# Mixer decay matrices from one spread matrix product and a ScalarE relu, causal mask moved into the scores, and the first norm's sums inside the first dense tile

## The chip, the cores and the metric

The kernel runs on one core of a Trainium2 chip. The core has TensorE (matrix products, in the profile PE, with its weight loads as PEld), VectorE (DVE), ScalarE (ACT) and GpSimd (POOL); each runs its own instruction list and waits for the others by semaphores. SyncE (SP) issues most DMAs. The metric is device time of one launch in microseconds (us), lower is better.

## The reference

One layer of a hybrid decoder: an RMSNorm, one wide input projection that feeds three branches, a gated merge, and a convolutional feed-forward. There are 512 prompt tokens and 8 x 8 sample tokens, so 576 columns in all. The change touches the first norm, the step sizes `dt` and the state-space mixer (branch a), which works in chunks of 128 tokens (the 64 sample tokens are a fifth, narrower chunk) for 32 heads in 8 groups of 4:

```python
def _rmsnorm(x, w):
    y = xf * lax.rsqrt(jnp.mean(xf * xf, axis=-1, keepdims=True) + RMS_EPS)
    return (y * w.astype(jnp.float32)).astype(x.dtype)

dt = jax.nn.softplus(dt_raw.astype(jnp.float32) + lw["dt_bias"].astype(jnp.float32))
a = -jnp.exp(lw["a_log"].astype(jnp.float32))
cs = jnp.cumsum((dt * a).reshape(b, c, chunk, h), axis=2)
seg = cs[:, :, :, None, :] - cs[:, :, None, :, :]
lmat = jnp.exp(jnp.where(causal[None, None, :, :, None], seg, -jnp.inf)).reshape(b, c, chunk, chunk, g, r)
cb = jnp.einsum("bcign,bcjgn->bcijg", cc, bc)
y_diag = jnp.einsum("bcijgr,bcjgrp->bcigrp", cb[..., None] * lmat, xdt)
```

Here i is the receiving token and j the source token. Because `dt * a` is negative, `cs` falls along a chunk, so `cs_i - cs_j` is at most 0 wherever j is at or before i.

## The kernel before

Features lie on the 128 partitions and tokens on the columns. Every projection is cut into dense tiles: 128 output features, 1024 inputs in 8 pieces of 128, 576 tokens in two halves of 288. Each fp32 operand is split in a high and a low part, so a tile is 48 matmuls of 288 columns (`pe_dense`; L208 and L213 where all pieces stand ready, L228 where it goes piece by piece). GpSimd splits the streamed weights (L2627, L2631), paced by the end of earlier tiles.

The order of work on each engine is written out by hand; there is no scheduler. TensorE's list is: the sums of the first norm, the step-size stage `pe_dt`, then the mixer.

**First norm and first tile.** ScalarE and GpSimd square the eight pieces of x. With `alone=5`, TensorE sums five squared pieces one by one and then the sum `acc` of the other three, which VectorE adds up (L385, L389): 30 products with one moving column (L287). The mean and its root follow on VectorE and ScalarE. The first dense tile (the step sizes) works on unnormed rows `y_hi`, `y_lo` and is scaled afterwards by the spread root (`pe_spread`, L310); `act_copied` (L375) and `dve_scaled` (L370) wait for the tile's end, and VectorE makes the normed rows only after that (L412, L365).

**Step-size stage.** VectorE computes `dt` and `dt * a`, lays the latter out for the cumulative sums (five copies, L1155), then runs the first convolutions (L920). TensorE makes the cumulative sums (L1073); ScalarE copies them into `cs_row` and `cs_lhs` (L1098, L1099), and VectorE subtracts to get their low parts (L1168, L1169). Then convolutions and SiLUs go on; the last SiLU (L936) frees the first chunk on TensorE (L551).

**Mixer.** For each of 8 groups G there are six slots. Slot k on TensorE is: a dense tile for the next group, from k = 2 on a state product (`pe_round`, L624), the products of chunk k (`pe_chunk_out`, L574 to L599), then the preparation of chunk k+1 (`pe_chunk`). The chunks of a group are `STEPS = (0, CH, 1, 2, 3)`, where CH is the narrow sample chunk. The preparation makes the scores and transposes in psA (L551 to L554), and, in two PSUM banks psL and psE of the tile psLE:

```python
            if c > 0:
                if s == 2:
                    pe.wait_ge(ysb_ready, G + 1)
                pe.matmul(per_head(psE[:, 0:GH * m]), ones_top[:], cs_rhs[:, :, 0:m], start=True, stop=True)
            late = late_p if c < CH else late_s
            pe.matmul(per_head(psL[0:m, 0:GH * m]), cs_lhs[:, at], cs_rhs[:, :, 0:m], start=True, stop=False)
            pe.matmul(per_head(psL[0:m, 0:GH * m]), eye_r[0:m, 0:m], over_heads(late[0:m, 0:m], m, m),
                      start=False, stop=True).then_inc(le_full, 1)
```

psE is cs_i spread over the partitions (L562), psL is cs_i - cs_j (L564) plus a large negative number where j is later than i (L565). On ScalarE a slot is: a copy (L714), the Exp of psL (L716) and of psE (L718), `act_rhs` for the next chunk (four copies with a per-partition scale, L706), the copies and first tap of a convolution (L751 to L756, L763), its tanh (L771). On VectorE: the chunk's outputs (L893 to L905), the scaled inputs (L871, L872), Exp times scores (L876), Exp times C (L880), the decay of sample states (L987), the convolution (L920), the state addition `dve_round` (L993), a SiLU (L935, L936). The banks psL and psE also take the state product L624, so `pe_chunk` waits for `n_free`, which L993 raises, ahead of the first matmul into them.

## Time and profile before

| | us |
|---|---|
| median of 3 runs | 1792.97 (1792.79 to 1794.67) |
| the profiled execution, its own time | 1796.09 |
| its span, first to last instruction | 1794.0 |
| TensorE busy | 1733.1 (97%) |
| VectorE busy | 939.3 (52%) |
| ScalarE busy | 621.0 (35%) |
| GpSimd busy | 977.2 (54%) |

The span is what the trace covers; 2.1 us of the execution's own time lie around it. Busy time is that of instructions, and a matmul's end is modelled, so neighbouring matmuls overlap in the rows: what one costs is the distance from its start to the next start. The mean granted TensorE clock was 0.986 of full speed. In a timeline row, "x4" merges four instructions in a row, and the bracket is the idle time ahead of it with what ended it.

### The profile page before, as it was taken

Reading aid. Unit: us, or ns where it says so; the run is one execution under the profiler, and the core shown is the slowest. Engines: PE = TensorE matmul, PEld = TensorE weight load, DVE = VectorE, ACT = ScalarE, POOL = GpSimd, SP = SyncE. Lnnn points to the kernel's source line nnn. Section 1 sums busy time; section 2 is a strip of 40 time slices with the busy share of each in tenths; the row PEclk is TensorE's granted clock in tenths of the full one; section 3 lists DMA queues with packets and bytes.
Section 4 is the critical chain, followed back from the end, with each engine's and each line's share of the span. In section 5 each row is a group of like instructions: output and inputs, shape, how many; then the busy total and the mean of one; then the engine's idle time right before and its main releaser. Section 6 shows DMA issues by size and latency. Waiting matters only on the chain.

```text
span 1794.0 us, 35603 instructions
## 1 busy us (share of the span) xinstructions
PE 1733.1 (97%) x13875; PEld 1603.1 (89%) x13875; DVE 939.3 (52%) x1584; ACT 621.0 (35%) x1660; POOL 977.2 (54%) x1088
## 2 busy tenths in 40 slices
PE   7899999999999999998998999999999999999997
PEld 7798898999898999786777998879998999999997
DVE  6766677631775424766664732222246651662454
ACT  3455555523554201555442112320124430331231
POOL 5535454555445466221553544236676876886775
PEclk9899999999999999999999999999999999999998
DMA  4212322313133223113895265532221222223223
GB/s 142 92 48 98 109 77 81 109 60 121 60 103 104 90 88 117 48 48 107 298 303 213 75 237 206 189 123 83 83 83 61 82 90 79 81 82 91 74 83 109
DMA packets 53605, 198.48 MB, mean 111 GB/s; under 512 B 6353, under 2 KB 7378, under 8 KB 49874
## 3 DMA queue, kind: packets, MB, share of 16 engines
q1 hardware_dynamic: 41762, 134.32, 22.9%
q10 hardware_dynamic: 7056, 46.85, 7.1%
q0 software_dynamic: 4640, 15.21, 2.6%
q8 instruction: 110, 1.80, 0.4%
q14 instruction: 37, 0.30, 0.1%
HBM read 180.43 MB, written 15.92 MB: 109 GB/s over the span
## 4 chain that ended last, share of the span: by engine, by line
PE 87%; DVE 6%; DMA 2%; ACT 2%; issue 1%; POOL 0%; SPq 0%; DVEq 0%; POOLq 0%; ACTq 0%
PE dps L208 36%; PE dps L213 18%; PE dps L228 14%; DMA pages<-kv_pages_dram 2%; PE psY L574 1%; PE psLE L1688 1%; PE psLE L624 1%; PE psY L591 1%; PE psY L287 1%; PE psLE L2135 1%; PE psY L1412 1%; PE psLE L2097 1%; DVE cout L920 1%; PE psY L1711 1%; PE psA L1402 1%
## 5 line engine op out<-in xcount | busy, mean ns | idle before, releaser
L2631 POOL TENSOR_TENSOR w_lo<-w_raw,w_hi 128x256 fp32r<-128x256 f32 x800 | 699.3, 905 | 16.7
L2627 POOL TENSOR_SCALAR w_hi<-w_raw 128x1024 fp32r<-128x1024 f32 x200 | 218.9, 1094 | 651.3 <-PE dps L213 385.2
L208 PE MATMUL dps<-xn_hi,w_hi 128*128 128x288 f32 x1504 | 323.3, 297 | 3.0 <-ACT cbuf L756 1.9
L208 PE MATMUL dps<-xn_lo,w_hi 128*128 128x288 f32 x1504 | 325.0, 298 | 0.0
L208 PEld LDWEIGHTS dps<-xn_hi,w_hi 128*128 128x128 f32 x1504 | 247.0, 190 | 6.0 <-POOL w_hi L2627 2.1
L208 PEld LDWEIGHTS dps<-xn_lo,w_hi 128*128 128x128 f32 x1504 | 241.5, 189 | 0.0
L213 PE MATMUL dps<-xn_hi,w_lo 128*128 128x288 f32 x1504 | 215.7, 296 | 0.0
L213 PEld LDWEIGHTS dps<-xn_hi,w_lo 128*128 128x128 f32 x1504 | 205.7, 189 | 0.0
L208 PE MATMUL dps<-y_lo,w_hi 128*128 128x288 f32 x824 | 177.9, 298 | 0.0
L208 PE MATMUL dps<-y_hi,w_hi 128*128 128x288 f32 x824 | 177.1, 297 | 0.5 <-POOL w_hi L2627 0.5
L228 PE MATMUL dps<-xn_hi,w_hi 128*128 128x288 f32 x624 | 144.5, 313 | 5.3 <-DVE xn_lo L365 4.5
L208 PEld LDWEIGHTS dps<-y_hi,w_hi 128*128 128x128 f32 x824 | 134.5, 190 | 0.9 <-POOL w_hi L2627 0.8
L228 PE MATMUL dps<-xn_hi,w_lo 128*128 128x288 f32 x624 | 134.8, 298 | 0.0
L228 PE MATMUL dps<-xn_lo,w_hi 128*128 128x288 f32 x624 | 134.3, 297 | 0.0
L208 PEld LDWEIGHTS dps<-y_lo,w_hi 128*128 128x128 f32 x824 | 132.9, 189 | 0.0
L228 PEld LDWEIGHTS dps<-xn_hi,w_hi 128*128 128x128 f32 x624 | 100.0, 191 | 30.2 <-issue 20.9
L213 PE MATMUL dps<-y_hi,w_lo 128*128 128x288 f32 x824 | 118.5, 296 | 0.0
L213 PEld LDWEIGHTS dps<-y_hi,w_lo 128*128 128x128 f32 x824 | 112.7, 189 | 0.2 <-POOL w_lo L2631 0.2
L920 DVE SCALAR_TENSOR_TENSOR cout<-cbuf,fea,cout 128x600 f32<-128x600 f32 x96 | 84.3, 879 | 42.1 <-ACT cout L763 39.6
L228 PEld LDWEIGHTS dps<-xn_lo,w_hi 128*128 128x128 f32 x624 | 101.6, 191 | 0.0
L228 PEld LDWEIGHTS dps<-xn_hi,w_lo 128*128 128x128 f32 x624 | 101.3, 190 | 0.0
L2514 DVE SCALAR_TENSOR_TENSOR fout<-fin,fea,fout 128x592 f32<-128x592 f32 x44 | 48.4, 1100 | 91.4 <-ACT fout L2500 91.4
(417 smaller groups left out, 2816.7 us busy)
## 6 DMA issues: line engine op xcount, KB each, us to landing
w_raw<-wstream_dram SPq DMA_DIRECT2D x209, 512.0 KB, 3.5
pages<-kv_pages_dram SPq DMA_DIRECT2D x70, 256.0 KB, 3.9
pages<-kv_pages_dram POOLq DMA_DIRECT2D x58, 256.0 KB, 4.1
st_in<-state_t_dram ACTq DMA_DIRECT2D x8, 1024.0 KB, 5.0
ssm_s_dram<-st_in ACTq DMA_DIRECT2D x8, 1024.0 KB, 4.3
kc<-mem_kt_dram ACTq DMA_DIRECT2D x4, 2048.0 KB, 7.9
vc<-mem_v_dram ACTq DMA_DIRECT2D x3, 2048.0 KB, 7.8
w_more<-wstream_dram SPq DMA_DIRECT2D x8, 512.0 KB, 3.8
```

Source lines behind the costliest of these rows:

```text
L208: pe.matmul(dps[:, par, b, 0:cw], w_hi[:, par, k * P:(k + 1) * P], a[:, k, c0:c0 + cw], start=(k == 0 and j == 0), stop=False)
L213: mm = pe.matmul(dps[:, par, b, 0:cw], w_lo[:, par, k * P:(k + 1) * P], hi[:, k, c0:c0 + cw], start=False, stop=(k == nk - 1))
L228: mm = pe.matmul(dps[:, par, b, 0:cw], w, a[:, k, c0:c0 + cw], start=(k == 0 and j == 0), stop=(k == nk - 1 and j == 2))
L287: mm = pe.matmul(psY[:, c * kinds + kind:c * kinds + kind + 1], squares[:, r], ones[:, 0:1], start=True, stop=True)
L574: pe.matmul(o, xdt[0:m, h * 64:h * 64 + 64], lv[:, h, :], start=True, stop=not carried)
L591: pe.matmul(psY[:, 256:512], btok[:], xdtd[:], start=True, stop=True).then_inc(y_full, 1)
L624: mm = pe.matmul(psLE[:, half, 0:256], bm[rows, half * 4 + r, :], xds[rows, :], start=True, stop=True)
L920: ins = dve.scalar_tensor_tensor(co, cb[:, j:j + CW - PAD], w(j), co, ALU.mult, ALU.add)
L1402: mm = pe.transpose(turn_bank(n)[:, k * P:(k + 1) * P], probs(i)[:, hh, kt * P:(kt + 1) * P], ident)
L2514: link(dve.scalar_tensor_tensor(fo, fb[:, 1:1 + FO], tap_of("fconvw", p, u, 1, FCONV), fo, ALU.mult, ALU.add))
L2627: pool.tensor_scalar(w_hi[:, par, :], w_raw[:, par, :], 1.0, 1.0, ALU.mult, ALU.mult).then_inc(w_hi_done, 1)
L2631: ins = pool.tensor_tensor(w_lo[:, par, at], w_raw[:, par, at], w_hi[:, par, at].bitcast(F32), ALU.subtract)
```

## The change

It does three things.

In the mixer, `cs_lhs`, the matrix `late` and its identity `eye_r` go away. Only psE is made, for every chunk. ScalarE forms `relu(cs_j - cs_i)` for each of the four heads, with psE as input, scale -1 and the source token's sum `cs_tok` as per-partition bias, waits for itself (`act_step`), and takes Exp with scale -1 in place. Tokens j later than i come out as some number up to 1, and the causal mask is multiplied into the scores on VectorE (`scores`), which the product with the four heads then reads instead of psA. The rows 64 to 127 of `cs_rhs` are set once to zero instead of once a group.

In the step-size stage, the layout copy becomes one copy of half the columns, the copies and subtractions for `cs_lhs` go away, and TensorE and ScalarE make `cs_tok`, two products and two copies.

In the first norm, `alone` is 2 instead of 5: VectorE adds up six squared pieces, the first two additions ahead of its first rows, and TensorE's sum over `acc` stands inside the first dense tile after its second piece; the spread stands after the sixth piece instead of the fifth. VectorE's constants, of which five go away, are made after the rows instead of first.

```diff
@@ norm_stage: pe_sums, dve_f
                 for k in range(alone):
-                    if k in POOL_SQUARED:
-                        pe.wait_ge(norm_lo_pool, k - POOL_SQUARED[0] + 1)
-                    else:
-                        pe.wait_ge(sq_ready, at["sq_ready"] + k + 1)
+                    pe.wait_ge(sq_ready, at["sq_ready"] + k + 1)
                     sums_of(pe, sq[:, k, :], k)
+                if not rows:
+                    pe_sum_last(pe)
+
+            def pe_sum_last(pe):
                 pe.wait_ge(sq_used, at["sq_used"] + adds)
                 sums_of(pe, acc, alone).then_inc(sum_full, 1)
...
                 if rows:
+                    dve.wait_ge(sq_ready, alone + 1)
+                    add(3)
+                    add(4)
                     dve_row_low(dve, 0)
                     dve_row_low(dve, 1)
                     dve_first_low(dve)
...
+                    for k in range(X_FIRST, KT):
+                        add(k)
+                    for k in range(2, 5):
+                        dve_row_low(dve, k)
...
@@ pe_chunk
-            if c > 0:
-                if s == 2:
-                    pe.wait_ge(ysb_ready, G + 1)
-                pe.matmul(per_head(psE[:, 0:GH * m]), ones_top[:], cs_rhs[:, :, 0:m], start=True, stop=True)
-            late = late_p if c < CH else late_s
-            pe.matmul(per_head(psL[0:m, 0:GH * m]), cs_lhs[:, at], cs_rhs[:, :, 0:m], start=True, stop=False)
-            pe.matmul(per_head(psL[0:m, 0:GH * m]), eye_r[0:m, 0:m], over_heads(late[0:m, 0:m], m, m),
-                      start=False, stop=True).then_inc(le_full, 1)
+            if s == 2:
+                pe.wait_ge(ysb_ready, G + 1)
+            pe.matmul(per_head(psE[:, 0:GH * m]), ones_top[:], cs_rhs[:, :, 0:m], start=True, stop=True).then_inc(le_full, 1)
@@ act_rhs, act_chunk
-            if s == 0:
-                act.activation(cs_rhs[64:P, :, :], spread(sel[64:P, group_heads(G)], 64, P), ACT.Copy)
+            if n == 0:
+                act.activation(cs_rhs[64:P, :, :], over_heads(ones[64:P, :], 64, P), ACT.Copy, scale=0.0)
...
-            ins = act.activation(l_exp[0:m, 0:GH * m], psL[0:m, 0:GH * m], ACT.Exp)
+            for h in range(GH):
+                at_h = slice(h * m, h * m + m)
+                ins = act.activation(l_exp[0:m, at_h], psE[0:m, at_h], ACT.Relu, bias=cs_tok[0:m, c, G * GH + h:G * GH + h + 1], scale=-1.0)
+            chains["act"](ins)
+            ins = act.activation(l_exp[0:m, 0:GH * m], l_exp[0:m, 0:GH * m], ACT.Exp, scale=-1.0)
@@ dve_chunk
+            causal = c_("upto_p") if c < CH else c_("upto_s", TS)
+            link(dve.tensor_tensor(scores[0:m, 0:m], psA[0:m, 384:384 + m], causal, ALU.mult))
             dve.wait_ge(exp_ready, n + 1)
             lv = per_head(l_exp[0:m, 0:GH * m])
-            ins = dve.tensor_tensor(lv, lv, over_heads(psA[0:m, 384:384 + m], m, m), ALU.mult)
+            ins = dve.tensor_tensor(lv, lv, over_heads(scores[0:m, 0:m], m, m), ALU.mult)
@@ pe_dt
-            pe_dense(pe, first, y_hi, y_lo, ready=rows_ready, part=(0, 5))
+            pe_dense(pe, first, y_hi, y_lo, ready=rows_ready, part=(0, 2))
+            norm1.pe_sum_last(pe)
+            pe_dense(pe, first, y_hi, y_lo, ready=rows_ready, part=(2, 6))
             norm1.pe_spread(pe)
-            pe_dense(pe, first, y_hi, y_lo, ready=rows_ready, part=(5, KT))
+            pe_dense(pe, first, y_hi, y_lo, ready=rows_ready, part=(6, KT))
...
+            pe.matmul(psL[:, 256:384], c_("upto_p"), da, start=True, stop=True)
+            pe.matmul(psL[0:TS, 384:416], c_("upto_s", TS), dt_tok[0:TS, 1, CH, :], start=True, stop=True)
@@ act_dt
-            for dst, r0 in ((cs_row[:], 0), (cs_lhs[64:P, :], 64)):
-                act.activation(dst[:, 0:SEQ], psY[r0:r0 + 64, :], ACT.Copy)
-                act.activation(dst[:, SEQ:T], psA[r0:r0 + 64, cs_tail], ACT.Copy).then_inc(cs_hi, 1)
+            act.activation(cs_row[:, 0:SEQ], psY[0:64, :], ACT.Copy)
+            act.activation(cs_row[:, SEQ:T], psA[0:64, cs_tail], ACT.Copy).then_inc(cs_hi, 1)
+            act.activation(cs_tok[:, 0:CH, :].rearrange("p c h -> p (c h)"), psL[:, 256:384], ACT.Copy)
+            chains["act"](act.activation(cs_tok[0:TS, CH, :], psL[0:TS, 384:416], ACT.Copy))
@@ dve_dt
-            for c in range(CH + 1):
-                p = P if c < CH else TS
-                four = dt_tok[0:p, 1, c, :].rearrange("p (o h) -> p o h", o=1).to_broadcast([p, 4, HEADS])
-                dve.tensor_copy(da_rows[0:p, c * P:(c + 1) * P].rearrange("p (o h) -> p o h", o=4), four)
+            dve.tensor_copy(da_rows.rearrange("p (c o h) -> p c o h", c=CH + 1, o=2),
+                            dt_tok[:, 1, :, :].rearrange("p c (o h) -> p c o h", o=1).to_broadcast([P, CH + 1, 2, HEADS]))
...
-            dve.wait_ge(cs_hi, 2)
-            for low, r0 in ((cs_row, 32), (cs_lhs, 96)):
-                part = low[r0:r0 + 32, :]
-                dve.tensor_tensor(part[:, 0:SEQ], psY[r0:r0 + 32, :], part[:, 0:SEQ].bitcast(F32), ALU.subtract)
-                ins = dve.tensor_tensor(part[:, SEQ:T], psA[r0:r0 + 32, cs_tail], part[:, SEQ:T].bitcast(F32), ALU.subtract)
-            ins.then_inc(cs_done, 1)
+            dve.wait_ge(cs_hi, 1)
+            low = cs_row[32:64, :]
+            dve.tensor_tensor(low[:, 0:SEQ], psY[32:64, :], low[:, 0:SEQ].bitcast(F32), ALU.subtract)
+            dve.tensor_tensor(low[:, SEQ:T], psA[32:64, cs_tail], low[:, SEQ:T].bitcast(F32), ALU.subtract).then_inc(cs_done, 1)
```

The diff moves instructions at three places. First, on TensorE from its first matmul: L287 is a sum over one squared piece or over `acc`, L228 the first dense tile. Before:

```order
L287 MATMUL psY<-cst,norm_sq 128x1 x25
L287 MATMUL psY<-cst,norm_acc 128x1 x5
L228 MATMUL dps<-y_hi,w_hi 128x288 x2
L228 MATMUL dps<-y_lo,w_hi 128x288 x2
L228 MATMUL dps<-y_hi,w_lo 128x288 x2
L228 MATMUL dps<-y_hi,w_hi 128x288 x2
L228 MATMUL dps<-y_lo,w_hi 128x288 x2
L228 MATMUL dps<-y_hi,w_lo 128x288 x2
```

After the change:

```order
L287 MATMUL psY<-cst,norm_sq 128x1 x10
L228 MATMUL dps<-y_hi,w_hi 128x288 x2
L228 MATMUL dps<-y_lo,w_hi 128x288 x2
L228 MATMUL dps<-y_hi,w_lo 128x288 x2
L228 MATMUL dps<-y_hi,w_hi 128x288 x2
L228 MATMUL dps<-y_lo,w_hi 128x288 x2
L228 MATMUL dps<-y_hi,w_lo 128x288 x2
L287 MATMUL psY<-cst,norm_acc 128x1 x5
L228 MATMUL dps<-y_hi,w_hi 128x288 x2
```

Fifteen of the thirty one-column sums are gone, and the five over `acc` stand behind the tile's first two pieces.

Second, on TensorE and ScalarE in the mixer, at the third chunk of a group. L551 to L554 (then L560 to L563) fill psA, L562 (then L570) is psE. TensorE before:

```order
L551 MATMUL psA<-feat 128x128
L553 MATMUL psA<-cst,feat 128x128 x2
L554 MATMUL psA<-cst,feat 128x128
L562 MATMUL psLE<-cs_rhs,ones_top 128x512
L564 MATMUL psLE<-cs_rhs,cs_lhs 128x512
L565 MATMUL psLE<-late_p,eye_r 128x512
L208 MATMUL dps<-xn_hi,w_hi 128x288 x2
```

TensorE after the change:

```order
L560 MATMUL psA<-feat 128x128
L562 MATMUL psA<-cst,feat 128x128 x2
L563 MATMUL psA<-cst,feat 128x128
L570 MATMUL psLE<-cs_rhs,ones_top 128x512
L208 MATMUL dps<-xn_hi,w_hi 128x288 x2
L208 MATMUL dps<-xn_lo,w_hi 128x288 x2
```

The two products into psL are gone and the next dense tile follows psE. ScalarE at the same chunk, before:

```order
L714 ACTIVATE btok<-psA 128x128
L716 ACTIVATE l_exp<-psLE 128x512
L718 ACTIVATE e_exp<-psLE 128x512
L706 ACTIVATE cs_rhs<-cs_row,sel 64x128 x4
L751 ACTIVATE cbuf<-dps 128x288
```

ScalarE after the change:

```order
L718 ACTIVATE btok<-psA 128x128
L722 ACTIVATE l_exp<-psLE,cs_tok 128x128 x4
L724 ACTIVATE l_exp<-l_exp 128x512
L726 ACTIVATE e_exp<-psLE 128x512
L710 ACTIVATE cs_rhs<-cs_row,sel 64x128 x4
L759 ACTIVATE cbuf<-dps 128x288
```

One Exp has become four relus and an Exp, all ahead of the Exp of psE and of the copies for the next chunk.

Third, on VectorE in the step-size stage, from `dt * a` (into `dt_tok`) to the first SiLU. Before:

```order
L1127 TENSOR_TENSOR dt_tok<-dt_tok,feat 128x160
L1155 COPY yg<-dt_tok 128x128 x4
L1155 COPY yg<-dt_tok 64x128
L1156 TENSOR_TENSOR ysb<-dt_tok,cst 64x256
L920 SCALAR_TENSOR_TENSOR cout<-cbuf,fea,cout 128x600 x6
L935 SCALAR_TENSOR_TENSOR feat<-cth,cout 128x512
```

After the change:

```order
L1136 TENSOR_TENSOR dt_tok<-dt_tok,feat 128x160
L1161 COPY yg<-dt_tok 128x320
L1163 TENSOR_TENSOR ysb<-dt_tok,cst 64x256
L930 SCALAR_TENSOR_TENSOR cout<-cbuf,fea,cout 128x600 x6
L945 SCALAR_TENSOR_TENSOR feat<-cth,cout 128x512
L946 SCALAR_TENSOR_TENSOR feat<-cth,cout 128x64
```

Five copies have become one of 320 columns, ahead of the six convolution steps.

## Rows read from the trace of the kernel before

**Rows 1.** The page: busy time by engine; the chain that ended last.

```profile
PE 1733.1 (97%) x13875; PEld 1603.1 (89%) x13875; DVE 939.3 (52%) x1584; ACT 621.0 (35%) x1660; POOL 977.2 (54%) x1088
...
PE 87%; DVE 6%; DMA 2%; ACT 2%; issue 1%; POOL 0%; SPq 0%; DVEq 0%; POOLq 0%; ACTq 0%
```

**Rows 2.** Timeline of TensorE around one chunk: start, length (us), instruction.

```profile
166.22 0.48 PE L562 MATMUL psLE<-cs_rhs,ones_top 128*128 128x512 f32 x1
...
176.19 0.48 PE L562 MATMUL psLE<-cs_rhs,ones_top 128*128 128x512 f32 x1
176.50 0.40 PE L564 MATMUL psLE<-cs_rhs,cs_lhs 128*128 128x512 f32 x1
176.74 0.39 PE L565 MATMUL psLE<-late_p,eye_r 128*128 128x512 f32 x1
176.97 0.42 PE L208 MATMUL dps<-xn_hi,w_hi 128*128 128x288 f32 x2
```

**Rows 3.** Waits of TensorE, whole span: us in total, times, longest.

```profile
PE psA L551 <- DVE feat L936: 6.1, 1, 6.1
...
PE dps L208 <- ACT cbuf L756: 1.9, 1, 1.9
```

**Rows 4.** Timeline of ScalarE, same step, part.

```profile
166.50 0.28 ACT L714 ACTIVATE btok<-psA 128x128 f32<-128x128 f32 x1 [3.31 <-PE psA L554]
167.20 0.60 ACT L716 ACTIVATE l_exp<-psLE 128x512 f32<-128x512 f32 x1 [0.42 <-PE psLE L565]
...
168.17 1.28 ACT L706 ACTIVATE cs_rhs<-cs_row,sel 64x128 fp32r<-64x128 f32 x4
...
170.37 0.89 ACT L763 ACTIVATE cout<-cbuf,fea 128x600 f32<-128x600 f32 x1
```

**Rows 5.** Timeline of VectorE, same step, part.

```profile
171.37 2.60 DVE L920 SCALAR_TENSOR_TENSOR cout<-cbuf,fea,cout 128x600 f32<-128x600 f32 x3 [0.98 <-ACT cout L763]
174.23 0.69 DVE L993 TENSOR_TENSOR st_in<-st_in,psLE 128x512 f32<-128x512 f32 x1 [0.26 <-PE psLE L624]
```

**Rows 6.** Timeline of TensorE from its first work to the second dense tile, part.

```profile
9.02 10.80 PE L287 MATMUL psY<-cst,norm_sq 128*128 128x1 f32 x50 [9.02 <-ACT norm_sq L325]
...
21.81 0.83 PE L228 MATMUL dps<-y_hi,w_hi 128*128 128x288 f32 x2
...
23.39 0.68 PE L228 MATMUL dps<-y_hi,w_hi 128*128 128x288 f32 x2
23.87 0.68 PE L228 MATMUL dps<-y_lo,w_hi 128*128 128x288 f32 x2
...
27.34 1.45 PE L310 MATMUL psLE<-cst,norm_rs 128*128 128x128 f32 x12
...
31.06 0.43 PE L208 MATMUL dps<-y_hi,w_hi 128*128 128x288 f32 x2
```

**Rows 7.** Timeline of VectorE in the same stretch, part.

```profile
13.83 1.97 DVE L1111 TENSOR_TENSOR w_lo<-w_raw,w_hi 128x1024 fp32r<-128x1024 f32 x1 [1.02 <-POOL w_hi L2685]
15.72 1.27 DVE L385 TENSOR_TENSOR norm_acc<-norm_sq 128x576 f32<-128x576 f32 x1
```

**Rows 8.** Timeline of VectorE in the step-size stage, part.

```profile
56.38 3.17 DVE L1155 COPY yg<-dt_tok 128x128 f32<-128x128 f32 x5
...
71.85 0.68 DVE L1168 TENSOR_TENSOR cs_row<-psY,cs_row 32x512 fp32r<-32x512 f32 x1 [0.86 <-ACT cs_lhs L1099]
...
72.68 0.70 DVE L1168 TENSOR_TENSOR cs_lhs<-psY,cs_lhs 32x512 fp32r<-32x512 f32 x1
...
73.55 3.45 DVE L920 SCALAR_TENSOR_TENSOR cout<-cbuf,fea,cout 128x600 f32<-128x600 f32 x3
```

**Rows 9.** Timeline of ScalarE in the step-size stage, part.

```profile
71.11 0.59 ACT L1098 ACTIVATE cs_lhs<-psY 64x512 fp32r<-64x512 f32 x1
```

**Rows 10.** Two stretches: length, busy time by engine, granted clock (PEclk), DMA share, GB/s.

```profile
73.70:80.40 6.70, 6.62 (x48) 6.41 (x48) 5.49 (x7) 2.00 (x3) 3.90 (x4) 1.00 0.22 66
86.40:89.75 3.35, 3.29 (x12) 3.09 (x13) 2.60 (x6) 1.24 (x4) 0.00 (x0) 0.50 0.49 157
```

59 lines of the change are left out of this document (26 added, 33 removed).

## Prediction

> **What bounds the kernel now.** I read the page first. TensorE is busy for 97% of the span, and 87% of the chain that ended last is TensorE's [rows 1]. So an instruction taken out of its list is worth its spacing, as long as nothing else becomes the last to be ready. The timeline of TensorE around one chunk shows the price: the two products into psL start at 176.50 and 176.74 and the next dense tile at 176.97, with no idle time noted, so 0.47 us for both. The same chunk step one slot earlier started at 166.22, this one at 176.19: a slot lasts 9.97 us [rows 2].
>
> The list of TensorE's waits has two long ones before the mixer's steady part: 6.1 us for VectorE's last SiLU (L936) and 1.9 us for a ScalarE copy (L756) [rows 3]. There VectorE and ScalarE set the time, not TensorE, and what counts is what leaves their lists. In the mixer I then read ScalarE and VectorE over the same slot, for the room that they have behind TensorE [rows 4, 5], and the start of all engines [rows 6, 7].
>
> **Mixer, TensorE.** Wide chunks 1 to 3 lose both products into psL: 24 times 0.47 = 11.3 us. Chunk 0 loses two and gains psE, so one: 8 times 0.23 = 1.8 us. The narrow chunk loses two of 256 columns; I have no row for these here, so the bounds are 0 and the 0.47 of the wide ones, and I take 0.40, near the wide ones, since a weight load stands with each: 8 times 0.40 = 3.2 us (0 to 3.8). Sum: 16.3 us.
>
> **Mixer, ScalarE.** The price is four relus with a per-partition bias and a wait, ahead of Exp. No relu is in the trace. The nearest row is L706, four 128-column activations with a per-partition scale: 1.28 us from the first start to the last end [rows 4]. A relu reads PSUM, L706 reads SBUF; L714, 128 columns out of PSUM without a per-partition operand, took 0.28 us, so PSUM is not dear. As bounds I take 0.28 us for the four together, as if they overlapped into one, and 0.60 us for each, the price of L716 at four times the width. I take 1.28 us, since L706 shares width and kind of operand.
>
> Let T be the start of psE (166.22 in the slot shown). L714 ends at T+0.56, the relus at T+1.84, the in-place Exp starts at T+1.87. The two Exps took 0.97 us together (167.20 to 168.17), so L706 starts at T+2.84, where before it started at T+1.95: ScalarE is 0.9 us later against psE. Behind it, L763 ended at T+5.04 (170.37+0.89) and now ends at T+5.93; the convolution L920 waits for it and started 0.1 us later; its three steps of 2.60 us end at T+8.63, and L993 (0.69 us), which stands behind it on VectorE, ends at T+9.33. The next psE waits for L993. Before, L993 ended at 174.92 and psE came at 176.19: 1.27 us of room [rows 2, 5]. After, psE would come at T+9.97-0.47 = T+9.50: 0.2 us of room, 0.1 with the way of a semaphore. This holds in slots 2 and 3 of the seven groups that have convolutions, so 14 times. The removed work thus fits, but only just: I put 1.0 us of loss in the sum, and the bounds are 0 (room kept) and, at 0.60 us a relu, 2.40-1.28-0.1 = 1.0 us, 14 times, 14 us.
>
> The masked scores on VectorE are one 128x128 product. They stand ahead of VectorE's wait for Exp, which now comes 0.9 us later, so they cost nothing; if ScalarE were early, they would cost at most as much as the state addition on 512 columns, 0.69 us, in 40 chunks, on an engine with time to spare at most of them. The product of scores and Exp stays as wide as it was. The zero rows of `cs_rhs` made once instead of eight times and the five constants off VectorE's list lie beside other work; I give them nothing. SP's and GpSimd's queues keep their order, and no DMA moves.
>
> **Step-size stage.** Five copies of 128 columns took 3.17 us [rows 8], 0.63 each. One of 320 columns, half as many elements, costs 1.6 us at the same rate; it costs no less than one of the five, 0.63 us. GpSimd works beside it as before, so part of the price is per instruction: I take 1.0 us, a gain of 2.2 us (1.6 to 2.5). ScalarE's copy for `cs_lhs` at 71.11 stood ahead of VectorE's subtraction at 71.85, which waited 0.86 us for it [rows 8, 9]: 0.74 us goes. The second pair of subtractions, 72.68 to the convolution at 73.55, goes: 0.87 us. The new copies of `cs_tok` stand behind the signal `cs_hi`, and the tanh behind them is not awaited for several us. Sum: 3.8 us (3.2 to 4.1). All of it reaches TensorE, since it waits 1.9+6.1 = 8.0 us there and its two added products, four instructions at the 1.45 us of the twelve of the spread [rows 6], take 0.5 us of that.
>
> The Trainium skill (VectorE: DVE Perf Modes, "Side-by-side: where the cycles go") counts a single-source copy in SBUF at two elements a cycle plus about 158 cycles at 0.96 GHz. By it the five copies would be an estimated 5 times 0.23 = 1.2 us and the new one 0.33 us, a gain of 0.8 us and a sum lower by 1.4 us. The trace has 3.17 us for the five, so I go by the row.
>
> **First norm.** The first dense tile now waits for w_lo (L1111, ends at 15.80 [rows 7]) instead of the thirty sums, so it starts at 15.8 instead of 21.81 [rows 6]. Two pieces, 12 matmuls, at the spacing of the first rows (0.48 us a pair, 0.24 each) end at 18.7. VectorE adds three pieces from 15.8 at 1.2 us each (L385 took 1.27), so `acc` is there at 19.5. Five sums are ten instructions at 10.80/50 = 0.216 us: until 21.7. So the sum, and the mean, come as late as before; what is gained is the two pieces already done and the spread at a better place.
>
> Then 36 matmuls and the spread remain. Before, 48 and a spread of about 1.4 us took 9.25 us (21.81 to 31.06). A matmul of the tile costs 0.24 us at the slow spacing and 0.138 at the fast one (6.62 us for 48 [rows 10]; a pair lasts 0.68 us at 23.39 and 0.43 at 31.06 [rows 6]), so about 12 of the 48 were slow, although TensorE had been busy with one-column sums since 9.02. I take it that 12 are slow again after the sums: 2.9+24 times 0.138+1.4 = 7.6 us, so the tile ends at 29.3 and with a short wait for rows at 29.5, a gain of 1.5 us. Bounds: all 36 fast, 6.4 us, gains 2.9; all slow with the spread doubled, 11.4 us, loses 2.0. The tile's end carries on undiminished, because `act_copied` and `dve_scaled` wait for it and VectorE's normed rows stand behind.
>
> **Sum.** 1.5+3.8+16.3-1.0 = 20.6 us. Against the profiled execution's 1796.09 that is 1775.5; its time was 3.1 us above the median of the runs, so for a median I forecast 1772.4, say 1772.
>
> **Rivals.** A change within 0.2% (3.6 us) is about what a measurement of this kernel cannot tell from none.
>
> *A. ScalarE's loop binds.* If a relu takes 0.42 us, four take 1.68 instead of 1.28, and the loop is 0.3 us over TensorE's slot. If slot 1, where eight masked copies and the copy of psE to `ysb` stand behind the relus, is as tight, that is 21 places and 6.3 us, 5.3 more than in the sum: 1778. For it: the room is 0.1 us, a small difference of many rows. Against it: L706. Chance 0.22.
>
> *B. The clock.* After the 6.1 us wait, 86.40 to 89.75 ran at a granted clock of 0.50, the lower of its two levels (1.2 GHz); after the 1.9 us wait, 73.70 to 80.40 had 1.00 [rows 10]. The new wait ahead of the first chunk is 8.0-3.8-0.5 = 3.7 us, between them. If the clock stays up, 3.35/2 = 1.7 us more are gained, and if the first tile's 36 matmuls are fast too, 1.4 more: 1769. Against it: the first tile began slow behind 12 us of sums. Chance 0.15. The Trainium skill (TensorE: Matmul & The Clock Gate, "HAM oscillation") says that idle gaps between groups of matmuls bring the clock back to half; the two rows agree, and do not say where a gap of 3.7 us falls.
>
> *C. Slower.* The same loop, with dearer relus. To lose 20.6+1.0+3.6 = 25 us in 14 slots, each must be 1.8 us over, the four relus 3.2 us, 0.8 us each: 1797 or more. That is above the 0.60 us of an activation four times as wide. It takes a stall in PSUM that no row shows. Chance 0.03.
>
> *D. No change.* The removed products would have to be covered by other work. Only a loop 1.5 us over TensorE's slot gives that, 0.73 us a relu: 1793. Chance 0.03.
>
> **How the numbers follow.** The forecast itself has 0.55 (1769 to 1775), A 0.22, B 0.15, C and D 0.03 each, and 0.02 is left for a first tile that loses its 2.0 us. The range 1767.5 to 1780 takes in A and B with their bounds and leaves out C and D. Faster by over 0.2%: 0.94; within: 0.03; slower: 0.03.
>
> **What would show it.** Right: in the profile after, dense matmuls start within 0.3 us of psE's start, slots 2 and 3 of a group are about 9.5 us apart, no wait of TensorE for L993's successor sums to more than 2 us, and the wait for the last SiLU is 3 to 4.5 us. Wrong: TensorE waiting for the state addition or for `ysb` by tenths in every slot (A), relus above 0.4 us apart, or the second dense tile starting later than 31.06.

## The result and the profile after

The changed kernel took 1782.11 us (median of 15 runs, 1766.16 to 1787.84), the kernel before 1793.22 in the same session; the ratio is 0.9927, 95% interval 0.991 to 0.9945. So it is faster, by 10 to 16 us as the interval has it, and not by the 20.6 of the forecast: 1782 lies above the range of 1767.5 to 1780.

The profiled execution took 1780.18 us, its span is 1778.5. Its page, lines on busy time and on the chain, as [rows 1]:

```profile
PE 1712.6 (96%) x13777; PEld 1584.4 (89%) x13777; DVE 963.1 (54%) x1616; ACT 655.9 (37%) x1813; POOL 979.7 (55%) x1088
...
PE 78%; DVE 8%; ACT 7%; DMA 3%; issue 3%; POOL 0%; ACTq 0%; DVEq 0%; POOLq 0%; SPq 0%
```

TensorE's busy time fell by 20.5 us. That this is close to the forecast's 20.6 means nothing, since part of the latter are waits. TensorE's share of the chain that ended last fell from 87% to 78%, and ScalarE's rose from 2 to 7: part of the work taken away turned into waiting. TensorE's waits in the mixer (total, times, longest), to be held against [rows 3]:

```profile
PE psA L560 <- DVE feat L946: 4.4, 1, 4.4
PE psY L660 <- DVE l_exp L886: 2.4, 6, 0.4
PE psLE L570 <- DVE st_in L1003: 1.7, 9, 0.2
```

The 6.1 us wait is 4.4, the 1.9 us wait for `cbuf` is gone, and L660 is new: it is the row that TensorE spreads between two groups (`pe_grow`). Where the difference between the two profiles arises can be read from the first product of each of the 40 chunks. Chunk (0, 0) starts at 83.10 instead of 86.46, 3.4 us earlier; the last chunk at 582.11 instead of 591.58, 9.5 earlier, so the mixer gave 6.1 of the 15.3 forecast (the second profiles of the two kernels give 2.7 to 6.8 for it). The other 6.0 us of the two spans' difference arise behind the mixer, where nothing was changed: from the last chunk to the end it is 1202.4 us before and 1196.4 after. Over all profiles of this study with the whole work in them that stretch lies between 1189.9 and 1204.6 us, and the three with the mixer of before (1198 to 1203) lie inside the range of the others, so these 6.0 us cannot be put down to the change. A spread of 15 us there is wide enough for most of the 14 to 22 us over which the runs of one kernel lie, though only one run in each set was traced. Effects of 1 to 4 us are therefore read below from places in the traces and not from medians alone.

Distance from each chunk's first product to the next one's, in us, median over the groups, from the timelines (0-1 is chunk 0 to chunk 1, 4-0 is chunk 4 to the next group's chunk 0; chunks are numbered in the order of `STEPS`, so chunk 1 is the narrow one). The forecast is before less its own terms, 0.23, 0.40 for the narrow chunk and 0.47 three times, without the loss of 1.0 us in all:

```
                                        0-1    1-2    2-3    3-4    4-0
before                                11.16  10.30  10.03   9.98  17.06
forecast                              10.93   9.90   9.56   9.51  16.59
after                                 11.77   9.85   9.56   9.88  16.99
after, second profile                 11.79   9.72   9.56   9.87  16.99
one relu for four heads               12.68   9.71   9.57   9.50  16.70
GpSimd's split cut                    11.78   9.71   9.57   9.51  16.60
three edits of order                  11.16   9.71   9.57   9.50  16.69
those, and products of constants      12.67   9.71   9.57   9.50  16.69
those, and chunk 0's product twice    11.16   9.71   9.57   9.50  16.70
```

Chunk 2 to 3 came out to the hundredth and 1 to 2 within 0.1. The loss is in 0-1 (0.84 us a group against the forecast), 3-4 (0.37) and 4-0 (0.40). The theory with which the experiments began: 0-1 waits for ScalarE's longer chain at the group boundary, 3-4 and 4-0 for VectorE's taps (the three convolution steps of a slot), which now meet GpSimd. The rivals: ScalarE's relus alone hold all of them (the prediction's A), or it is chance of one execution.

### The profile page after: what moved, and what is told of

The parts are those of the page before. It is cut to its first block, busy times and chain, and to the rows that moved or that the text cites. A ratio compares the mean times of both kernels' runs of the same rounds, so it can differ in the third digit from the quotient of the medians.

```text
span 1778.5 us, 35636 instructions
## 1 busy us (share of the span) xinstructions
PE 1712.6 (96%) x13777; PEld 1584.4 (89%) x13777; DVE 963.1 (54%) x1616; ACT 655.9 (37%) x1813; POOL 979.7 (55%) x1088
## 4 chain that ended last, share of the span: by engine, by line
PE 78%; DVE 8%; ACT 7%; DMA 3%; issue 3%; POOL 0%; ACTq 0%; DVEq 0%; POOLq 0%; SPq 0%
PE dps L208 34%; PE dps L213 17%; PE dps L228 12%; DVE cout L930 2%; DMA ssm_p_dram<-state 1%; PE psLE L1693 1%; DMA pages<-kv_pages_dram 1%; ACT l_exp L722 1%; ACT cs_rhs L710 1%; PE psY L1417 1%; ACT cout L771 1%; PE psY L1716 1%; PE psLE L2140 1%; PE psA L1407 1%; PE psLE L2102 1%
## 5 line engine op out<-in xcount | busy, mean ns | idle before, releaser
L2636 POOL TENSOR_TENSOR w_lo<-w_raw,w_hi 128x256 fp32r<-128x256 f32 x800 | 697.4, 903 | 16.7
L2632 POOL TENSOR_SCALAR w_hi<-w_raw 128x1024 fp32r<-128x1024 f32 x200 | 223.5, 1117 | 634.8 <-PE dps L213 363.5
L228 PE MATMUL dps<-xn_hi,w_hi 128*128 128x288 f32 x624 | 143.5, 312 | 4.3 <-DVE xn_lo L363 3.9
L228 PE MATMUL dps<-xn_hi,w_lo 128*128 128x288 f32 x624 | 134.9, 298 | 0.0
L228 PE MATMUL dps<-xn_lo,w_hi 128*128 128x288 f32 x624 | 134.4, 297 | 0.0
L228 PEld LDWEIGHTS dps<-xn_hi,w_hi 128*128 128x128 f32 x624 | 100.3, 192 | 27.8 <-issue 20.9
L930 DVE SCALAR_TENSOR_TENSOR cout<-cbuf,fea,cout 128x600 f32<-128x600 f32 x96 | 104.6, 1090 | 31.4 <-ACT cout L771 28.9
L228 PEld LDWEIGHTS dps<-xn_hi,w_lo 128*128 128x128 f32 x624 | 101.5, 191 | 0.0
L228 PEld LDWEIGHTS dps<-xn_lo,w_hi 128*128 128x128 f32 x624 | 101.5, 191 | 0.0
```

The source lines that it names most:

```text
L228: mm = pe.matmul(dps[:, par, b, 0:cw], w, a[:, k, c0:c0 + cw], start=(k == 0 and j == 0), stop=(k == nk - 1 and j == 2))
L930: ins = dve.scalar_tensor_tensor(co, cb[:, j:j + CW - PAD], w(j), co, ALU.mult, ALU.add)
L2632: pool.tensor_scalar(w_hi[:, par, :], w_raw[:, par, :], 1.0, 1.0, ALU.mult, ALU.mult).then_inc(w_hi_done, 1)
L2636: ins = pool.tensor_tensor(w_lo[:, par, at], w_raw[:, par, at], w_hi[:, par, at].bitcast(F32), ALU.subtract)
```

## The experiments

Times are medians against the kernel before on the same chip; a ratio has its 95% interval. The runs lie on four chips, so medians are set against each other below only where they come from one.

| kernel | us | ratio to before |
|---|---|---|
| changed kernel again | 1783.93 | 0.9951 (0.9934 to 0.9969) |
| kernel before again (one run) | 1792.2 | |
| mixer part only | 1784.39 | 0.9971 (0.9947 to 0.9996) |
| first norm only | 1790.59 | 0.9995 (0.9973 to 1.0016) |
| products ahead of the first tile | 1779.76 | 0.9937 (0.9916 to 0.9959) |
| spread row waits for scores | 1785.76 | 0.9969 (0.9948 to 0.999) |
| copied rows late | 1779.13 | 0.9927 (0.9897 to 0.9957) |
| GpSimd's split cut (work left out) | 1763.14 | 0.9831 (0.9809 to 0.9853) |
| one relu (biases left out) | 1779.02 | 0.9912 (0.9883 to 0.9941) |
| three edits of order | 1777.06 | 0.9918 (0.9905 to 0.993) |
| those, and products of constants | 1775.43 | 0.9913 (0.9882 to 0.9944) |
| those, and chunk 0's product twice | 1774.53 | 0.9896 (0.9878 to 0.9914) |
| changed kernel, chunk 0's product twice | 1782.76 | 0.9943 (0.9924 to 0.9962) |

**The taps.** VectorE, GpSimd and TensorE of the changed kernel in slot 2 of group 2, timeline (start, length, instruction). VectorE:

```profile
227.38 3.26 DVE L930 SCALAR_TENSOR_TENSOR cout<-cbuf,fea,cout 128x600 f32<-128x600 f32 x3 [0.26 <-ACT cout L771]
230.56 0.67 DVE L1003 TENSOR_TENSOR st_in<-st_in,psLE 128x512 f32<-128x512 f32 x1
```

And GpSimd at the same time:

```profile
228.59 1.42 POOL L2632 TENSOR_SCALAR w_hi<-w_raw 128x1024 fp32r<-128x1024 f32 x1 [3.45 <-PE dps L213]
230.09 4.00 POOL L2636 TENSOR_TENSOR w_lo<-w_raw,w_hi 128x256 fp32r<-128x256 f32 x4
```

TensorE, with the psE of the slot before as its first line:

```profile
221.49 0.47 PE L570 MATMUL psLE<-cs_rhs,ones_top 128*128 128x512 f32 x1
...
230.97 0.27 PE L563 MATMUL psA<-cst,feat 128*128 128x128 f32 x1
231.38 0.47 PE L570 MATMUL psLE<-cs_rhs,ones_top 128*128 128x512 f32 x1
231.69 0.42 PE L208 MATMUL dps<-xn_hi,w_hi 128*128 128x288 f32 x2
```

The kernel before, GpSimd in the slot of [rows 5]:

```profile
173.78 1.10 POOL L2627 TENSOR_SCALAR w_hi<-w_raw 128x1024 fp32r<-128x1024 f32 x1 [4.61 <-PE dps L213]
```

The three taps take 3.26 us instead of the 2.60 of [rows 5]. In the kernel before they ended at 173.97, and GpSimd began its split at 173.78, when the third was under way; now they start later in the slot and the split, which follows the dense tile, starts earlier. The third tap, begun at 229.1, takes 1.50 us; the two ahead of it 0.84. What counts is which begins first: in the changed kernel's mixer all 28 taps that begin during a conversion `w_hi` take 1.50 to 1.58 us, and the 28 that are under way when one begins keep their 0.84. The addition L1003 then ends at 231.2, and psE, which waits for it, comes at 231.38, 0.41 us behind the transpose before it; in the kernel before the distance is 0.03. It is 0.40 to 0.43 in both slots 2 and 3 of all seven groups with convolutions, 14 places. The list of waits shows little of this, because it counts a wait from the modelled end of the matmul ahead; 1.2 of its 1.7 us for L570 are a wait of 0.2 us at six group boundaries, and the kernel before has these too.

Edit 1, ScalarE's copy of the next chunk's rows (L710, 1.2 us) behind the first tap in slots 2 and 3:

```diff
-            if k < 4:
+            if k < 4 and k not in (2, 3):
                 act_rhs(act, G, k + 1)
...
                     act_conv(act, N, k - 1)
+                if k in (2, 3):
+                    act_rhs(act, G, k + 1)
```

> The changed kernel, but in slots 2 and 3 of a group ScalarE copies the next chunk's rows (cs_rhs) behind the first tap of the convolution instead of ahead of it, so that VectorE's other three taps can start about 1.1 us earlier. Theory (the taps now start so late that they run beside GpSimd's split of the next weights, which stretches them from 2.60 to 3.26 us, and the addition behind them holds up TensorE's spread product): the taps take 2.6 us again, TensorE's wait of 0.37 us for the addition goes in slots 2 and 3, the distances of chunks 2 to 3 and 3 to 4 fall to about 9.2 and 9.5 us; some 5 us over the mixer, about 1777 us. Rival (GpSimd has no part in it, the taps are slower beside ScalarE's relus or by their own operands): the taps still take about 3.26 us wherever they start; the wait goes all the same since they start earlier. Second rival (the copied rows are now late instead): TensorE waits for cs_rhs, and the distances stay at 9.56 and 9.88.

Half of it came. 3-4 fell to 9.51 and 4-0 to 16.7, and the mixer shortened by 3.7 us (495.32 instead of 499.01 from the first chunk to the last). But the taps stayed long (3.3 us): against the chunk's start they begin only 0.4 us earlier (5.98 us behind it instead of 6.41), because VectorE itself is busy until then, and the third one still met the split. 2-3 had nothing to give, it stood at the forecast already. So the taps were moved enough to clear TensorE's wait, not enough to clear GpSimd, and this run alone does not tell the theory from the first rival.

Edit 2, the split itself:

```diff
+            full = D if first else 64
-            pool.tensor_scalar(w_hi[:, par, :], w_raw[:, par, :], 1.0, 1.0, ALU.mult, ALU.mult).then_inc(w_hi_done, 1)
+            pool.tensor_scalar(w_hi[:, par, 0:full], w_raw[:, par, 0:full], 1.0, 1.0, ALU.mult, ALU.mult).then_inc(w_hi_done, 1)
...
-                at = slice(piece * D // 4, (piece + 1) * D // 4)
+                at = slice(piece * full // 4, (piece + 1) * full // 4)
```

> The changed kernel with GpSimd's split of the streamed weights cut to 64 of 1024 columns behind the first two tiles: the high and low parts of the other columns stay those of an earlier tile, so most of that work is left out; every other instruction stays. Theory (the taps are stretched only where they meet GpSimd: 1.5 us beside the high part, 1.2 beside the low parts, 0.84 alone): all taps take 0.84 us, three of them 2.6, TensorE's wait for the addition behind them goes, chunk 3 to 4 falls from 9.88 to about 9.5 us and chunk 4 to the next chunk 0 from 16.99 to about 16.7; chunk 0 to 1 stays at 11.77 (that wait is ScalarE's). Rival (ScalarE's longer chain alone sets these slots, GpSimd has no part): the taps take 0.84 us but the distances stay at 9.88 and 16.99. Second rival (the taps are slow by themselves): they still take 1.5 us.

The taps from 83 to 600 us, all instructions of the line (minimum, median and maximum in ns, first and last start). The changed kernel:

```profile
L930 DVE SCALAR_TENSOR_TENSOR cout<-cbuf,fea,cout x84: 842/844/1580, 102.3 to 532.6; 128x600 f32<-128x600 f32 x84
```

With the split cut:

```profile
L930 DVE SCALAR_TENSOR_TENSOR cout<-cbuf,fea,cout x84: 842/844/860, 94.6 to 522.5; 128x600 f32<-128x600 f32 x84
```

Without GpSimd no tap is longer than 0.86 us, 3-4 is 9.51, 4-0 is 16.60, and 0-1 stays at 11.78. That is the theory in every row: the stretch is GpSimd's, and the boundary is not. (Its time, 1763, is that of a kernel with much of GpSimd's work gone and is no goal; chunk (0, 0) also came 5 us earlier, since VectorE's step-size stage meets the split too: its first six taps take 5.14 us without it, 7.31 with it.) The Trainium skill has the rule that the prediction should have weighed (GPSIMD Engine Reference, "1. Specifications"): GpSimd shares its way into SBUF with VectorE, and contends with instructions of VectorE with two inputs in SBUF. A tap has two, and the trace agrees with 0.84 us alone and 1.5 beside `w_hi`.

Edit 3, the other engine of the same loop, one relu of 512 columns for four:

```diff
-            for h in range(GH):
-                at_h = slice(h * m, h * m + m)
-                ins = act.activation(l_exp[0:m, at_h], psE[0:m, at_h], ACT.Relu, bias=cs_tok[0:m, c, G * GH + h:G * GH + h + 1], scale=-1.0)
-            chains["act"](ins)
+            chains["act"](act.activation(l_exp[0:m, 0:GH * m], psE[0:m, 0:GH * m], ACT.Relu, bias=cs_tok[0:m, c, G * GH:G * GH + 1], scale=-1.0))
```

> The changed kernel with one relu of 512 columns in place of four of 128, all with the first head's source sum as bias: the other three heads' biases are left out. Theory (ScalarE's longer chain is what holds the row between two groups, and it is only one of the two things that cost the later chunks): with some 0.5 us less of it, chunk 0 to 1 falls from 11.77 to about 11.3 us, chunk 3 to 4 stays at 9.8 or above since the taps still meet GpSimd's split, 4 us less at most and about 1780 us. Rival (the relus alone held the later chunks, GpSimd's part follows from them): chunk 3 to 4 falls to 9.5 and chunk 4 to the next 0 to 16.7 as well, about 1776 us.

Here the rival is borne out on the later chunks: 3-4 is 9.50 and 4-0 is 16.70 although taps still reach 1.57 us. So either half is enough: the loop is 0.4 us too long, GpSimd put 0.66 us into it and the relus 0.9, and whoever takes 0.4 out of it clears the wait. The wait at L660 went too (0.2 us in all). But 0-1 did not fall: it is 12.68 to 12.71 in all of groups 1 to 4, 6 and 7. Neither case expected that; it is taken up below.

**The group boundary.** The changed kernel between groups 1 and 2, timelines. ScalarE:

```profile
202.73 1.14 ACT L722 ACTIVATE l_exp<-psLE,cs_tok 128x128 f32<-128x128 f32 x4
203.88 1.28 ACT L724 ACT_TABLE_LOAD   x1
...
205.18 0.63 ACT L724 ACTIVATE l_exp<-l_exp 128x512 f32<-128x512 f32 x1
```

VectorE:

```profile
203.86 0.28 DVE L883 TENSOR_TENSOR scores<-psA,cst 128x128 f32<-128x128 f32 x1
205.91 0.69 DVE L886 TENSOR_TENSOR l_exp<-l_exp,scores 128x512 f32<-128x512 f32 x1 [1.77 <-ACT l_exp L724]
```

TensorE's first instruction of `pe_grow`:

```profile
206.75 0.62 PE L660 MATMUL psY<-cst,grs 128*128 128x128 f32 x4 [0.44 <-DVE l_exp L886]
```

The kernel before, ScalarE at such a boundary:

```profile
147.45 0.26 ACT L714 ACTIVATE btok<-psA 128x128 f32<-128x128 f32 x1
147.73 1.28 ACT L716 ACT_TABLE_LOAD   x1
...
149.03 0.60 ACT L716 ACTIVATE l_exp<-psLE 128x512 f32<-128x512 f32 x1
```

The square root of the group ahead makes ScalarE load the table of the exponential anew, before the change too. Now the four relus stand ahead of that load, so load and exponential come 1.1 us later, and L886 behind them signals `m_ready`, on which `pe_grow` waits. It waits only because psA, which it writes, was read last by that product; since the change the last reader is L883, done 2.4 us earlier.

```diff
-            link(dve.tensor_tensor(scores[0:m, 0:m], psA[0:m, 384:384 + m], causal, ALU.mult))
+            dve.tensor_tensor(scores[0:m, 0:m], psA[0:m, 384:384 + m], causal, ALU.mult).then_inc(a_neg, 1)
+            dve.wait_ge(a_neg, n + 2)
...
-                pe.wait_ge(m_ready, G * 5 + 6)
+                pe.wait_ge(a_neg, G * 5 + 7)
```

> The changed kernel, but the row that TensorE spreads between two groups (pe_grow) waits for the masked scores of the next chunk, the last reader of the psA bank, instead of for the finished products of that chunk (m_ready). Theory (the group boundary now waits for the longer ScalarE chain of relus, table load and exponential): TensorE's 0.6 us in front of that row goes in seven of eight groups, and the distance from chunk 0 to chunk 1 falls from 11.77 us to about 11.2; some 4 us over the mixer, so about 1778 us median against 1782 of the changed kernel. Rival (slot 0 is held by something behind that row too, the state's start or the normalised feature, which is equally late): the wait moves to the next instruction, the distance stays within 0.2 us of 11.77 and the time stays 1782.

0-1 fell to 11.17, as the theory has it, but 1-2 rose to 10.46, and the time did not fall. The two longest of TensorE's waits in its mixer:

```profile
PE psA L560 <- DVE feat L947: 4.4, 1, 4.4
PE psLE L614 <- DMA st_in<-state_t_dram: 4.4, 5, 1.8
```

The gain went one slot on: the states of the next group are loaded by a DMA that waits for the store of the old ones, and ScalarE issues that store behind chunk 0's relus, at 261.04 in this profile for the boundary whose chunk 0 began at 256.43 (in the kernel before at 147.40, where it began at 144.23). The third edit issues it ahead of the square root. The diff of that edit, run with the two others:

```diff
                 if G:
+                    act_state_out(act, G - 1)
                     act_root(act, G - 1)
...
-            if k == 0 and G:
-                act_state_out(act, G - 1)
```

> The changed kernel with three edits of order: the copied rows behind the first tap in slots 2 and 3; the row spread between two groups waits for the masked scores instead of the finished products; and the DMA that writes the old states out is issued ahead of ScalarE's square root and relus of chunk 0 instead of behind them, some 2 us earlier. Theory (the second edit alone gained 0.6 us of each boundary and lost it to the load of the next states, 0.5 to 1.8 us late behind the store): chunk 0 to 1 falls to 11.17, chunk 1 to 2 stays at about 9.7 to 9.9, chunk 3 to 4 at 9.5, chunk 4 to the next 0 at 16.7; the mixer shortens by some 3.7 + 4 us against the changed kernel, about 1775 us. Rival (the store's issue ahead of the square root delays it and with it the whole boundary): chunk 4 to the next chunk 1 grows by 0.5 us or more, and the time is 1780 or above.

All distances are as the theory says, and of the waits behind chunk (0, 0) only 1.2 us at L570 are left. The mixer took 491.36 us instead of 499.01, the time is 1777.06 where the changed kernel on the same chip had 1783.93, and the intervals of the two ratios do not meet.

**The first norm.** Undone alone in the changed kernel (the diff, with the parts of `norm_stage` that belong to it), and the reverse of it alone in the kernel before:

```diff
-            pe_dense(pe, first, y_hi, y_lo, ready=rows_ready, part=(0, 2))
-            norm1.pe_sum_last(pe)
-            pe_dense(pe, first, y_hi, y_lo, ready=rows_ready, part=(2, 6))
+            pe_dense(pe, first, y_hi, y_lo, ready=rows_ready, part=(0, 5))
             norm1.pe_spread(pe)
-            pe_dense(pe, first, y_hi, y_lo, ready=rows_ready, part=(6, KT))
+            pe_dense(pe, first, y_hi, y_lo, ready=rows_ready, part=(5, KT))
```

> The changed kernel with the first norm of before (all sums ahead of the first dense tile, the constants of VectorE first): the first norm's part of the change undone alone. Theory (that part gives nothing, since in both orders the first tile's slow matmuls end at about the same time): the second dense tile starts within 0.3 us of 31.0 us and the time is that of the changed kernel, 1782 us within its noise of 2. Rival, the forecast (moving the sums is worth 1.5 us): the second dense tile starts 1.5 us later than in the changed kernel.

> The kernel before with the first norm of the changed kernel: that part alone. Theory: the second dense tile starts within 0.3 us of 31.06 us, and the time is that of before, 1793 us within 2. Rival, the forecast: the second tile starts at 29.6 us and the time is 1791.5. A third case, that the order is worth something only without the other edits' constants in VectorE's way: the second tile starts later than 31.06, by up to 1 us, since here the five constants that the change removes stand behind the sums.

The second tile started at 32.42 in the one, where the rival had 32.5, and at 27.66 in the other, 2 us earlier than its rival had. By their times neither shows a gain: the first norm alone stands at 0.9995 of the kernel before, and the interval of the kernel without it overlaps that of the changed kernel's second set. And the unchanged kernels once more:

> The changed kernel once more, unchanged, on the same chip as the three others, to measure them against and to see how much of its first norm is the luck of one execution. Theory (where TensorE's spacing falls in the first tile differs from one execution to the next, so one profile cannot size that term): the median is within 3 us of 1782, and the second dense tile starts either at about 31.0 or at about 27.7 us. Rival (it is set by the order of the program): 31.0 again, as in three of the four profiles with this order so far.

> The kernel before once more, for its trace: how much of the first tile and of the group boundaries is the luck of one execution. Theory: the spacing in the first tile falls somewhere between 24.8 and 27.7 us, the second tile starts between 31.0 and 32.5; one chunk 0 to 1 distance in seven or fewer shows the additional 1 to 1.5 us (12.7 instead of 11.2) that in the changed kernel's profiles stands at one to four of seven. Rival: these are set by the program, and both are as in the first profile, 24.8, 31.06, and one boundary, that of group 3.

Together these show what kind of term it is. With the old order the second tile started at 31.06, 31.61 and 32.42 in three profiles. With the new one it was 30.92 to 31.26 in seven and 27.66 and 27.68 in two. The two kinds differ in one thing, TensorE's spacing. The kernel that has the first norm alone, its timeline:

```profile
19.27 0.59 PE L228 MATMUL dps<-y_hi,w_lo 128*128 128x288 f32 x2
20.33 1.28 PE L287 MATMUL psY<-cst,norm_acc 128*128 128x1 f32 x10 [0.46 <-DVE norm_acc L385]
21.46 0.52 PE L228 MATMUL dps<-y_hi,w_hi 128*128 128x288 f32 x2
```

and the changed kernel:

```profile
19.32 0.68 PE L228 MATMUL dps<-y_hi,w_lo 128*128 128x288 f32 x2
20.37 2.30 PE L287 MATMUL psY<-cst,norm_acc 128*128 128x1 f32 x10 [0.37 <-DVE norm_acc L385]
22.53 0.83 PE L228 MATMUL dps<-y_hi,w_hi 128*128 128x288 f32 x2
```

In the first the clock rose just ahead of the sums, which then take 1.28 us instead of 2.30, and the 36 matmuls behind them are fast; in the second it rose at 27.5. The mean over the nine is 30.3 against 31.7 over the three, so 1.4 us, near the forecast of 1.5. But the three of the old order alone lie 1.4 apart, and the gain comes in lumps: nothing against the kernel before's first profile in seven executions, 3.4 us in two. To see whether it is the clock, three products of constants went into the 3.3 us wait ahead of the tile:

```diff
+            for _ in range(3):
+                pe.matmul(psE[:, 0:288], ones, cst[:, 0:288], start=True, stop=True)
             pe_dense(pe, first, y_hi, y_lo, ready=rows_ready, part=(0, 2))
```

> The changed kernel with three products of constants (288 columns each, into a bank that nobody reads at that time) between the first column sums and the first dense piece, where TensorE waits 3.28 us; nothing else. Theory (the first norm's part gave nothing since the slow spacing of 0.24 us lasts until 27.5 us: the first piece alone is too short to bring the spacing down ahead of the sums at 20.4 us, and behind them it starts anew): with the wait filled the spacing falls to 0.13 us ahead of 20 us, and the second dense tile starts at 27.7 us, as in the one profile in which it fell early, instead of 31.0; the time falls by up to 3 us, to about 1779. Rival (the rows of the first tile pace TensorE, not its clock): the second tile starts at 31.0 whatever the spacing. Second rival (a wait of VectorE or the weights behind the first tile takes the gain back): the second tile starts at 27.7 and chunk (0, 0) still starts at 83.1.

The spacing fell at 18.9, ahead of the sums, and rose again from 22.3 to 25.6. The second tile started at 29.10 and chunk (0, 0) at 81.19 instead of 83.1: 1.9 us, half of what was hoped, carried through undiminished. So it is the clock and not the rows, and no later wait takes it back. Its time, 1779.76 beside 1783.93 for the changed kernel on that chip, points the same way, but the intervals overlap.

**Where the clock falls.** Nine products of the same kind, in `pe_mixer` ahead of `pe_chunk(pe, 0, 0)`, went into the 4.4 us wait ahead of chunk (0, 0) as well, on top of the three edits:

> The kernel with the three edits of order, and products of constants in two waits of TensorE: three ahead of the first dense tile, as tried alone, and nine behind the last dense tile of the step-size stage, where TensorE waits 4.4 us for chunk (0, 0)'s features; nobody reads them. Theory (both gaps are followed by slow spacing that costs TensorE time): the second dense tile starts at 27.7 to 29.1 us instead of 31; chunk (0, 0)'s first product takes 0.38 instead of 0.79 us, and chunk 0 to 1 of group 0 falls from 10.0 to about 8.5 us as in the profile in which that gap was absent; together some 3 us below the 1777 us of the three edits, about 1774. Rival (what follows the second gap is paced by the vector and scalar engines, not by TensorE's clock): chunk 0 to 1 of group 0 stays at about 10 us, and the time is 1775 to 1777.

The clock behind that place is now granted in full (1.00 instead of 0.50), and chunk 0 to 1 of group 0 fell from 10.02 to 8.66, as expected. But in the other groups it was 12.7 at five of six boundaries, as with the one relu. The one-relu kernel at such a boundary, two stretches: the ten one-column products (L649), and what follows (length, busy TensorE, granted clock, DMA share, GB/s):

```profile
138.10:139.30 1.20, 1.17 (x11) 1.00 0.07 14
139.30:142.80 3.50, 3.50 (x16) 0.53 0.44 138
```

No wait is in the second: TensorE is busy throughout and runs 3.5 us at the lower level, which costs 1.5 us. The same boundary, TensorE's timeline ahead of and behind the ten:

```profile
137.56 0.48 PE L570 MATMUL psLE<-cs_rhs,ones_top 128*128 128x512 f32 x1 [0.21 <-DVE st_in L1000]
138.13 1.28 PE L649 MATMUL psY<-cst,feat 128*128 128x1 f32 x10
139.27 0.63 PE L228 MATMUL dps<-xn_hi,w_hi 128*128 128x288 f32 x2
139.69 0.68 PE L228 MATMUL dps<-xn_lo,w_hi 128*128 128x288 f32 x2
```

And in the kernel before:

```profile
145.25 0.47 PE L564 MATMUL psLE<-cs_rhs,cs_lhs 128*128 128x512 f32 x1 [0.21 <-DVE st_in L993]
145.56 0.40 PE L565 MATMUL psLE<-late_p,eye_r 128*128 128x512 f32 x1
145.83 1.28 PE L645 MATMUL psY<-cst,feat 128*128 128x1 f32 x10
146.97 0.51 PE L228 MATMUL dps<-xn_hi,w_hi 128*128 128x288 f32 x2
```

I counted boundaries with 12.6 us or more in groups 1 to 4, 6 and 7 of every profile. With the mixer of before: 1 of 18 (one, none, none). With the changed mixer: 29 of 60 (1 and 3 in the changed kernel's two, 1 to 6 in the eight others). At that place the order of TensorE differs in one thing: before, two products of 512 columns stood between the transposes and the ten one-column ones, now one. The ten start 0.58 us behind the first product either way, so one product, which alone would be followed after 0.31 us, leaves some 0.27 us in which TensorE has nothing new.

```diff
+            if G and s == 0:
+                pe.matmul(per_head(psE[:, 0:GH * m]), ones_top[:], cs_rhs[:, :, 0:m], start=True, stop=True)
             pe.matmul(per_head(psE[:, 0:GH * m]), ones_top[:], cs_rhs[:, :, 0:m], start=True, stop=True).then_inc(le_full, 1)
```

> The kernel with the three edits and the products of constants in two waits, and chunk 0's spread product issued twice in groups 1 to 7 (the same product into the same bank, so that two products of 512 columns stand ahead of the ten one-column products, as before the change; there is a wait of 0.3 us there that covers it). Theory (the product that the change took away kept TensorE's clock up over the one-column products): slow stretches behind them at no more than one of the six boundaries of groups 1 to 4, 6 and 7, instead of five of six; chunk 0 to 1 at 11.17 us nearly everywhere; the mixer 5 times 1.5 us shorter, and the time about 1770 us. Rival (where the clock falls is chance, or set by something else that the change moved): three to six of six boundaries still show 12.7 us, and the time stays at about 1775. Second rival (the second product is not covered): 0.23 us more from chunk 4 to chunk 1 at each boundary.

> The changed kernel with that one edit alone. Theory: chunk 0 to 1 stays at 11.77 us (the wait for the finished products is not touched) with a slow stretch at no more than one of six boundaries; the time falls by 1 to 4 us, to about 1779. Rival (chance): one to four of six boundaries slow as in the two profiles of the changed kernel, 1782 us.

No boundary was slow in either, 0 of 12. The first of them at the same boundary, its timeline:

```profile
137.70 0.48 PE L571 MATMUL psLE<-cs_rhs,ones_top 128*128 128x512 f32 x1 [0.21 <-DVE st_in L1012]
138.02 0.40 PE L572 MATMUL psLE<-cs_rhs,ones_top 128*128 128x512 f32 x1
138.28 1.27 PE L651 MATMUL psY<-cst,feat 128*128 128x1 f32 x10
```

The stretches:

```profile
138.20:139.50 1.30, 1.30 (x12) 1.00 0.92 384
139.50:143.00 3.50, 3.50 (x28) 1.00 0.63 234
```

The second product costs nothing: the ten products start 0.58 us behind the first one, as they did in the changed kernel (200.37 to 200.95) and before. It adds columns and fills the 0.27 us at once; the runs do not tell which of the two holds the clock up. The mixer took 487.02 us, 18 less than before and 12 less than the changed kernel. The time is 1774.53, the lowest of the study with the whole computation, and 8.2 us below the changed kernel with the doubled product on the same chip; its interval overlaps those of the two kernels that it is built on, and the 1770 that was expected did not come. The other run shows the limit of the edit: its time did not fall as expected, 1782.76. Without the waits mended, 0-1 is 11.77 everywhere, a slow stretch costs it only 0.9 us since it hides the wait, the load of the states took 3.0 us of waits, and its mixer is 499.38, not shorter than the 499.01 of the first profile and 3 us shorter than the 502.40 of the second.

## Why the prediction was right and wrong

The direction and most single terms held. Dense matmuls start 0.31 us behind a wide psE (231.38 to 231.69); the 0.47 us of a wide chunk is what 2-3 lost; the four relus take 1.14 us (1.28 taken), so A's condition of 0.42 us each is false; the masked scores take 0.28 us on VectorE, which still waits 0.26 us for ScalarE ahead of the taps, so they cost nothing. The narrow chunk was worth more than the 0.40 taken and than its bound of 0.47: in the kernels with the waits mended 1-2 is 9.71, 0.58 us less than before.

**Step-size stage**, 3.8 forecast: VectorE's convolution starts at 70.02 instead of 73.55, 3.5 earlier. The new copy took 0.49 us, where I took 1.0 from the row and the Trainium skill's page (VectorE: DVE Perf Modes, "Side-by-side: where the cycles go") gave an estimate of 0.33: the page was nearer. From the second tile to chunk (0, 0) it was 55.4 and 54.4 us in the two profiles of before and 52.1 in both of after, so 2.3 to 3.3 arrived. VectorE in the changed kernel:

```profile
56.43 0.49 DVE L1161 COPY yg<-dt_tok 128x320 f32<-128x320 f32 x1
...
69.17 0.68 DVE L1174 TENSOR_TENSOR cs_row<-psY,cs_row 32x512 fp32r<-32x512 f32 x1
...
70.02 2.60 DVE L930 SCALAR_TENSOR_TENSOR cout<-cbuf,fea,cout 128x600 f32<-128x600 f32 x3
```

The five old copies in the second profile of the kernel before:

```profile
57.02 0.76 DVE L1155 COPY yg<-dt_tok 128x128 f32<-128x128 f32 x5
```

Here they take 0.76 us in all, 0.21 to 0.23 each, not the 3.17 of [rows 8], and GpSimd begins its split only at 58.22; in the first profile it began at 56.11, ahead of the copies. So the row from which the term was sized was one beside GpSimd, and the gain from the copies is 2.7 us or 0.3 us as they meet it or not. The page's estimate of 0.23 us for one of them agrees with the copies that stand alone.

**First norm**, 1.5: 0.06 in the profiled execution; that the mean over executions comes near it is luck. The tile started at 16.76, not at 15.8, since the two rows of `y_lo` ahead of w_lo took 3.10 us, where they took 1.53 in the kernel before. And "12 are slow again after the sums" holds in no profile without added products: there it is none or some 20.

**The mixer**, 16.3 less 1.0, is where the forecast failed, in three places.

1. The step that failed is "its three steps of 2.60 us end at T+8.63": it took the taps at the price of a slot in which they ran alone. Up to them the prediction's times hold. In the slot shown T is 221.49 and the taps start at T+5.89, where it had T+6.03. They took 3.26 us, ended at T+9.15, and the next psE came at T+9.89 instead of T+9.50. ScalarE's delay, which I had, moved them under GpSimd's split. The loop is then 0.4 us over in slots 2 and 3 instead of 0.1 under: 14 times 0.38, some 5.3 us, where I had put 1.0. The bound of 14 us came from a dearer relu, so the size was inside it for a cause I did not name. The loop binds, as rival A had it, but not by the relus. Of the signs, slots 2 and 3 were not 9.5 us apart but 9.9; the listed wait for L993's successor stayed under 2 us (1.7) all the same, for the reason given above, and was no good sign.
2. I looked at what is queued behind Exp on VectorE in the steady slots only. At the boundary a table load stands between relus and Exp, and `pe_grow` waits for what follows: 0.6 us at six boundaries, 3.7 us. The new scores product made that wait needless, and nothing used it.
3. Chunk 0's 0.23 us, 1.8 in all, was covered: what follows starts 0.58 us behind the first wide product in both kernels. And the product taken away there kept the clock up over the ten one-column products; that it could cost the clock was no case of mine. One and three boundaries pay 0.9 us for it in the changed kernel's two profiles.

What the mixer gave in the first profiles, before less after, summed over the groups, in us (the forecast without its loss of 1.0; the last chunk's 0.47 lies behind this stretch):

```
                                       0-1   1-2   2-3   3-4   4-0    sum
forecast                               1.8   3.2   3.8   3.8   3.3   15.9
changed kernel                        -4.0   3.3   3.7   1.1   2.0    6.1
all edits, chunk 0's product twice     3.5   4.7   3.7   4.1   2.3   18.1
```

Of the 5.9 us missing in 0-1, 1.8 are place 3's covered product and 3.7 place 2; the rest is the slow stretches and chunk 0 of group 0, which differ between two executions. 3-4 and 4-0 are place 1; from the last chunk of group 4 to the first of group 5, 72 us apart, the kernel before happened to be 1.6 us longer, which hides part of it in 4-0. The last line gives 14.7 us outside 0-1, where the forecast has 14.1: the work taken away was worth what the forecast put on it, once nothing else is ready last, and TensorE has 89% of the chain there. Its 3.5 us in 0-1 are the slow boundary of before (1.5) and group 0, whose clock the filled wait holds up (1.8).

Rival B was wrong in its hope: behind the 4.4 us wait TensorE starts slow again, at a granted clock of 0.50 from 83.1 to 86.5, its first two products taking 0.80 us as before. The Trainium skill (TensorE: Matmul & The Clock Gate, "HAM oscillation") names idle gaps between groups of matmuls; the 4.4 us wait agrees with it. At the group boundary there is no gap of that size: the clock falls behind products of one column, with waits of 0.2 and some 0.27 us ahead of them.

Not settled: why the slow boundaries vary from 1 to 6 of six between kernels that share that stretch of TensorE's order, whether the columns or the filled 0.27 us hold the clock there, and what spreads the part behind the mixer by 15 us.

## What to carry to other kernels

When an edit moves one engine's work later inside a slot, lay the rows of the engines that share memory with it beside the new place, not the old one: a price read from a row holds only with the row's neighbours, and a second profile can show the same row without them. Follow each signal that the lengthened chain gives to every waiter, at the boundaries of the loop too, and ask whether the edit has made the wait needless. Work taken from TensorE in front of narrow products can lower its clock; a product in a covered wait is free and can hold it up.

## What the runs showed of the hardware

- A VectorE instruction with two inputs in SBUF (128x600, 0.84 us alone) takes 1.50 to 1.60 us when it begins during GpSimd's conversion of 1024 columns and 1.20 beside its subtractions; one under way when the conversion begins keeps its 0.84. GpSimd's conversion takes up to 1.47 us in the changed kernel's mixer instead of 1.05.
- Five VectorE copies of up to 128x128 with one input take 0.76 us alone and 3.17 beside GpSimd's split (two profiles of the kernel before).
- Ten one-column products, 1.28 us, were followed by 3.5 us at the lower clock in 29 of 60 cases with one product of 512 columns ahead of them (and 0.27 us of TensorE's time unfilled), and in 1 of 30 with two (18 of before's mixer, 12 with the doubled product).
- In the first tile the granted clock is listed as 1.00 up to 27 us where the spacing of 0.24 us says the lower level; the spacing is the surer sign until the first change is on record.
